# Hybrid decoder step, expert layer: shorter routing, ranked experts with their own capacities, outputs scattered to tokens' places

## What is computed

```python
lg = (t @ w_rg) + b_rg                      # 4 groups
g = argmax(lg); p_top = softmax(lg)[g]
le = (t @ w_re[g]) + b_re[g]                # 4 experts of the group
top_v, top_i = top_k(le, 2)
w2 = softmax(top_v) * p_top
hid = silu(t @ w_gate[e]) * (t @ w_up[e])   # 1024 -> 256, 16 experts
out = sum over the two experts of w2 * (hid @ w_down[e])
x = x + out;  y = rmsnorm(x)
```

## Time and profile before

| | us |
|---|---|
| median of 3 runs | 1096.22 (1095.71 to 1102.13) |
| the profiled execution | 1102.08 |
| its span, first to last instruction | 1100.3 |
| PE busy | 881.9 (80%) |
| DVE busy | 661.7 (60%) |
| ACT busy | 426.6 (39%) |
| POOL busy | 230.9 (21%) |

### The profile page before, as it was taken

One profiled execution on the slowest core, in us unless ns is written; L12 is line 12 of the kernel. 1 busy time (PEld: TensorE's weight loads), 2 busy tenths in 40 slices (PEclk: granted clock), 3 DMA queues, 4 the chain that ended last, 5 costly groups with the idle time before them and its releaser, 6 DMA issues.

```text
span 1100.3 us, 16526 instructions
## 1 busy us (share of the span) xinstructions
PE 881.9 (80%) x6294; PEld 569.4 (52%) x6294; DVE 661.7 (60%) x1001; ACT 426.6 (39%) x744; POOL 230.9 (21%) x174
## 2 busy tenths in 40 slices
PE   5999897698899999648999699801899999999500
PEld 3766442264566443326666355401777887787300
DVE  5614754848655301767883333385488888888266
ACT  5420211545504101546664223460364555464121
POOL 2108965404120000300000000043111011100053
PEclk9999997889979999688999899955899999999855
DMA  8237763000212488400001222192688889872275
GB/s 299 43 95 243 245 214 125 0 25 15 61 60 78 146 260 286 164 8 1 2 1 39 77 77 79 40 311 76 226 304 296 288 300 323 287 273 99 73 269 183
DMA packets 100533, 164.78 MB, mean 150 GB/s; under 512 B 12954, under 2 KB 62634, under 8 KB 100466
## 3 DMA queue, kind: packets, MB, share of 16 engines
q1 hardware_dynamic: 92642, 138.10, 37.9%
q0 software_dynamic: 6208, 22.09, 6.1%
q10 hardware_dynamic: 1616, 3.70, 0.9%
HBM read 136.36 MB, written 27.51 MB: 149 GB/s over the span
## 4 chain that ended last, share of the span: by engine, by line
PE 56%; DVE 20%; issue 6%; ACT 5%; DMA 5%; POOL 4%; SPq 3%; POOLq 0%; ACTq 0%; DVEq 0%
PE ps L1933 15%; PE ps L1934 14%; PE ps L1935 14%; DVE w_reg L1323 2%; POOL kv L796 2%; DVE mxs L1585 2%; PE ps L2210 2%; DVE kv L1742 1%; ACT hT_reg L1213 1%; PE ps L2107 1%; DMA w_reg<-y_scratch,yrow 1%; PE ps L2282 1%; POOL rst L824 1%; SPq L630 1%; PE ps L2074 1%
## 5 line engine op out<-in xcount | busy, mean ns | idle before, releaser
L1933 PE MATMUL ps<-hT_reg,w_reg 128*128 128x344 f16 (+1 forms) x312 | 99.7, 319 | 4.6 <-DVE hT_reg L1335 2.7
L1933 PE MATMUL ps<-hT_reg,mix_reg 128*128 128x208 f16 x384 | 98.7, 257 | 4.8 <-DVE hT_reg L1815 4.8
L1934 PE MATMUL ps<-hT_reg,w_reg 128*128 128x344 f16 (+1 forms) x312 | 99.6, 319 | 0.0
L1935 PE MATMUL ps<-hT_reg,w_reg 128*128 128x344 f16 (+1 forms) x312 | 99.3, 318 | 0.0
L1934 PE MATMUL ps<-hT_reg,mix_reg 128*128 128x208 f16 x384 | 98.7, 257 | 0.0
L1935 PE MATMUL ps<-hT_reg,mix_reg 128*128 128x208 f16 x384 | 98.6, 257 | 0.0
L796 POOL TENSOR_TENSOR kv<-kv,mix_reg 128x1024 f32<-128x1024 f32 x32 | 82.4, 2604 | 47.8 <-DMA kv<-in_cache_k 47.8
L1933 PE MATMUL ps<-w_reg,hT_reg 128*128 128x512 f16 (+1 forms) x216 | 83.7, 387 | 4.9 <-DVE w_reg L1323 3.2
L1934 PE MATMUL ps<-w_reg,hT_reg 128*128 128x512 f16 (+1 forms) x216 | 83.4, 386 | 0.0
L1935 PE MATMUL ps<-w_reg,hT_reg 128*128 128x512 f16 (+1 forms) x216 | 83.1, 385 | 0.0
L824 POOL TENSOR_TENSOR rst<-rst,neghalf 128x1 f32<-128x1 f32 (+3 forms) x27 | 18.9, 702 | 254.9 <-DVE rst L1573 254.9
(11 more groups left out here) (376 smaller groups left out, 2245.5 us busy)
## 6 DMA issues: line engine op xcount, KB each, us to landing
kv<-in_cache_k SPq DMA_DIRECT2D x64, 256.0 KB, 3.4
w_reg<-in_w_gate SPq DMA_DIRECT2D x16, 1024.0 KB, 5.6
w_reg<-in_w_up SPq DMA_DIRECT2D x16, 1024.0 KB, 8.2
w_reg<-in_w_down SPq DMA_DIRECT2D x16, 1024.0 KB, 10.6
w_reg<-in_w_in SPq DMA_DIRECT2D x12, 1024.0 KB, 6.8
mix_reg<-in_cache_v SPq DMA_DIRECT2D x32, 256.0 KB, 3.2
kv<-in_cache_v SPq DMA_DIRECT2D x32, 256.0 KB, 3.1
y_scratch<-kv SPq DMA_DIRECT2D x16, 512.0 KB, 4.0
```

What stands on the lines that cost most here:

```text
L1933: pe.matmul(out, lh, rh, start=start, stop=False)
L1934: pe.matmul(out, lh, rl, start=False, stop=False)
L1935: return pe.matmul(out, ll, rh, start=False, stop=stop)
```

## The change

In words, by place:

- **Output projection**: SyncE loads gate and up of expert 0 before it; ScalarE rounds them at tiles 2 and 5, VectorE splits them at tiles 3 and 8. GpSimd splits only gate and up of expert 1. The constants of routing are made at tile 7.
- **Routing**: no mask of valid tokens, one product for both choices, `r_a16` in f16; prefix sums over tiles by ten matmuls (`strict16`, `ones16`) into one PSUM bank; place and column come out of one number `r_q`; gates, overflow counts and `oexp` come after the token table, behind the first token reads. The token table holds t+1 for a first choice and -(t+1) for a second; `tok` is its absolute value, `dest` the row in `y_scratch` (2 x 1032 rows).
- **Ranking**: experts 0 to 2 stay first at capacity 208; the other 13 are ranked by count in slots of capacity 212, 200, 188, 176, 164, 152, 140 and six of 128 (one part only); SyncE reads their numbers from `sexp`.
- **Slots**: written out, no loop; all widths by `CAPS[e]`; sigmoid as exp, ln, exp on ScalarE in place of plus one and reciprocal on VectorE; one part, 12 matmuls, of down where the capacity is 128; GpSimd stores y by indirect DMAs, `scatter`.
- **The end**: y lies by token, so SyncE loads it by plain DMAs; GpSimd has only the powers left.

```diff
+FIXED = 3
+CAP_TOP, CAP_STEP = 212, 12
+CAPS = [208] * FIXED + [max(P, CAP_TOP - CAP_STEP * j) for j in range(NE - FIXED)]
+def parts(e):
+    return [(0, P), (1, more(e))] if more(e) > 0 else [(0, P)]
@@ SyncE
+            sp.wait_ge(s_wol, KC // 2)
+            load_gate_up(0)
...
+            for t in range(NT + 1):
+                sp.dma_start(yg[t][0:rows(t)],
+                             yd.rearrange("(c t) d -> t c d", c=2)[P * t:P * t + rows(t)]).then_inc(y_in[t][0], 16)
@@ GpSimd
-            for part in range(2):
-                pool.wait_ge(s_mh2, part + 1)
-                split_first(s_mlo, 0, part)
-            pool.wait_ge(s_mhd, 1)
-            split_first(s_mld, 0, 2)
+            def scatter(e):
+                pool.wait_ge(s_ya, e + 1)
+                pool.wait_ge(s_yv, e + 1)
+                for g, r in parts(e):
+                    pool.indirect_dma_start(out=yd[:, :], out_offset=bass.IndirectOffsetOnAxis(
+                        ap=dest[0:r, 2 * e + g:2 * e + g + 1], axis=0), in_=yb[0:r, e % 2, D * g:D * g + D],
+                        in_offset=None, bounds_check=2 * T - 1, oob_is_err=False).then_inc(s_yo[e % 2], 16)
+            pool.wait_ge(s_rtr, NT + 2)
             gather(0)
             gather(1)
             for part in range(2):
                 pool.wait_ge(s_mh2, part + 3)
                 split_first(s_mlo, 1, part)
-            for e in range(2, NE):
-                gather(e)
+            pool.wait_ge(s_route, 1)
+            for e in range(NE):
+                if e + 2 < NE:
+                    gather(e + 2)
+                scatter(e)
@@ ScalarE, slot
+                    act.activation(g, gate_up(e)[0], ACT.Exp, scale=-ISC2).then_inc(s_sg, 1)
+                    act.wait_ge(s_sg, 3 * e + 1)
+                    act.activation(g, g, ACT.Ln, bias=1.0).then_inc(s_sg, 1)
+                    act.wait_ge(s_sg, 3 * e + 2)
+                    act.activation(g, g, ACT.Exp, scale=-1.0).then_inc(s_sg, 1)
                     if e != NE - 1:
+                        read_tokens(e + 1, 0)
+                        read_tokens(e + 1, 2)
@@ VectorE, routing after the counts
-            for t in range(NT + 1):
-                link(dve.tensor_tensor(r_pos[:, t], r_pos[:, t], r_ne, ALU.add))
-                link(dve.tensor_tensor(r_ne, r_ne, ps[:, 1, 16 * t:16 * t + 16], ALU.add))
+            link(dve.scalar_tensor_tensor(r_key, n_all, float(NE), iof[:, 0:NE], ALU.mult, ALU.subtract))
+            link(dve.tensor_tensor(r_beat[:, 0:nd, 0:nd], r_key[:, FIXED:].unsqueeze(1).to_broadcast([P, nd, nd]),
+                                   r_key[:, FIXED:].unsqueeze(2).to_broadcast([P, nd, nd]), ALU.is_gt))
+            link(dve.tensor_reduce(r_sl[:, FIXED:], r_beat[:, 0:nd, 0:nd], AX, ALU.add))
...
+            link(dve.scalar_tensor_tensor(r_sq, n_pos, SCL, per_expert(r_base), ALU.mult, ALU.add))
+            link(dve.scalar_tensor_tensor(r_sq, r_d, float(CAP_TOP), r_sq, ALU.is_ge, ALU.add))
+            chosen(r_sq, r_q)
@@ VectorE, slot
+                    if e != NE - 1:
+                        read_tokens(e + 1, 1)
+                    dve.wait_ge(s_sg, 3 * e + 3)
...
+                    for g, r in parts(v):
+                        dve.wait_ge(s_down, downs(e - 2) + 2 * g + 2)
+                        ins = dve.tensor_scalar(yb[0:r, v % 2, D * g + 512:D * g + D], ps[0:r, 5 + 2 * g, :], ISC2, None,
+                                                ALU.mult)
+                    ins.then_inc(s_yv, 1)
...
+                if e + 2 < NE:
+                    split_gate_up(e + 2, 0)
+                    split_gate_up(e + 2, 1)
+                if e + 1 < NE:
+                    split_down(e + 1)
@@ TensorE, counts
-            pe.matmul(ps[:, 0, 0:144], strict[:], r_a2, start=True, stop=True)
-            pe.matmul(ps[:, 1, 0:144], ones[:], r_a2, start=True, stop=True).then_inc(s_rc, 1)
+            pe.matmul(ps[:, 6, 0:160], strict16[:], r_a16.rearrange("p t e -> p (t e)"), start=True, stop=False)
+            for t in range(NT + 1):
+                ins = pe.matmul(ps[:, 6, 16 * (t + 1):160].rearrange("p (t e) -> p t e", e=16), ones16[:],
+                                r_a16[:, t].unsqueeze(1).to_broadcast([P, 9 - t, 16]), start=False, stop=t == NT)
+            ins.then_inc(s_rc, 1)
```

More of the change, by code:

```diff
@@ L102, with more, y_sent, downs @@
 PB = 4
+def more(e):
+    return CAPS[e] - P
+def parts(e):
+    return [(0, P), (1, more(e))] if more(e) > 0 else [(0, P)]
+def y_sent(e):
+    return 16 * sum(len(parts(k)) for k in range(e % 2, e + 1, 2))
+def downs(e):
+    return sum(2 * len(parts(k)) for k in range(e + 1))
+def one_bank(e):
+    return 4 * CAPS[e] <= 512
 def unit_banks():
@@ L478, in build @@
         r_tmp = work(18, 16)
-        r_a, r_pos = work(9, 16), work(9, 16)
-        r_ne, r_oc, r_inc, r_ost = [work(16) for _ in range(4)]
+        r_beat = r_tmp[:, 0:16]
+        r_d, r_sq, r_w = [work(9, 16) for _ in range(3)]
+        r_a16 = work(80).bitcast(F16).rearrange("p (t e) -> p t e", t=10)
+        r_key, r_sl, r_capm, r_base, r_oc, r_inc, r_ost, r_se = [work(16) for _ in range(8)]
         r_thr = work(8)
@@ L483, in build @@
         r_cmj = work(NOV, 16)
-        r_r, r_e, r_o, r_g, r_f, r_q, r_p, r_c, r_po, r_co, r_x, r_y = [work(18) for _ in range(12)]
-        r_q3 = work(18, 8)
-        r_tv = work(18)
+        r_q, r_qc, r_tv = [work(18) for _ in range(3)]
+        r_v, r_neg, r_none = [work(COLS) for _ in range(3)]
+        iof_p = work(P)
+        iof_c = work(COLS)
         oneh_p = work(18 * P // 2).bitcast(F16).rearrange("p (n q) -> p n q", n=18)
@@ L562, in when_overflow @@
                 body()
-        def run_slots(eng, slot):
-            for e in range(3):
-                slot(0, e, e)
-            with eng.Fori(1, NE // 2 - 2) as i:
-                slot(i, 1)
-                slot(i, 2)
-            for e in range(NE - 3, NE + 1):
-                slot((e - 1) // 2, e - 2 * ((e - 1) // 2), e)
         block = ctx.enter_context(nc.Block())
@@ L1257, in overflow @@
+            split_down(0, 16)
+            act.wait_ge(s_mw[1], 32)
+            for dst, src, _ in expert_parts(1, 0)[0:2]:
+                act.activation(dst, src, ACT.Copy, scale=SC)
+                act.activation(src, src, ACT.Copy, scale=SC).then_inc(s_mh2, 1)
+            read_tokens(0, 0)
+            read_tokens(0, 2)
+            for e in range(NE + 1):
+                slot(e)
             def overflow():
@@ L1773, in _ @@
[L1773 to L1781 removed]
+            link(dve.tensor_scalar(r_ost, r_ost, float(P), 1.0 - CAP_TOP, ALU.mult, ALU.add))
@@ L2266, in _, with transpose_tokens @@
+            ins.then_inc(s_rc, 1)
             for n in range(18):
+                r = rows(n % 9)
                 pe.wait_ge(s_rs1, n // 9 + 1)
-                ins = pe.matmul(ps[:, 2, 0:COLS], oneh_p[:, n], oneh_c[:, n], start=n == 0, stop=n == 17)
+                ins = pe.matmul(ps[:, 7, 0:COLS], oneh_p[0:r, n], oneh_c[0:r, n], start=n == 0, stop=n == 17)
             ins.then_inc(s_rsu, 1)
-            pe.wait_ge(s_route, 1)
-            def transpose_tokens(s, loaded, e4, e2):
-                pe.wait_ge(s_gx[s], loaded)
+            def transpose_tokens(e):
+                s, c, r = e % 2, CAPS[e], more(e)
+                pe.wait_ge(s_gx[s], y_sent(e))
```

629 lines of the change are left out of this document (332 added, 297 removed).

## The result

Four runs of the changed kernel took 1178.65 to 1183.31 us, median 1182.36, beside 1096.47 for the kernel before: a ratio of 1.0755, 95% interval 1.0709 to 1.080. The change costs 86 us. I had forecast slower, and 1113 us; the measured time lies 50 us above the upper end of my range.

What follows compares the result with a forecast made beforehand. Slots were taken as bound by TensorE, routing as a VectorE chain. Routing -27.3, slots +58.8 and the end -14.9 sum to +16.6 us, 1118.7 for the profiled execution, scaled to 1113 us; 8-in-10 range 1050 to 1132.

Steps and rivals of the forecast that it cites:

- What bounds the kernel: Kernel before: routing is one chain on VectorE; expert slots are bound by TensorE, at work 239 of 255 us.
- the routing chain: Routing on VectorE: first gather at 733.8 instead of 758.5, -24.9 us; -27.3 up to the second expert's gate and up end.
- its cost of 0: Output projection: the added copies and splits cost 0, since TensorE sets the pace; 4 us if the cover were gone.
- The loop through GpSimd: Slots: scatters queued ahead of gathers close a loop; a large slot takes 23.2 us instead of 16.05, +58.8 in all.
- Y: In a slot, the end of VectorE's last read of y, forecast 10.4 us after the transposes' start.
- scatters end at 3.1 and 5.3, the first gather at 7.5, the second starts at 7.8 and lands 5.0 later at the least: Large slot, GpSimd's queue after VectorE's last y read, slowed by its splits: rows land 12.8 us after that read.
- Y + 15: Large slot: the gather's landing if weight loads delay it, 15 us after VectorE's last y read instead of 12.8.
- slots 2 to 8: The seven slots with two scatters and two gathers in the loop, 23.2 us each, 162.4 us together.
- The end: From the last expert's gate and up to the kernel's end: shorter down, plain loads of y; -14.9 us from 79.
- (a): Slots: GpSimd's order binds but VectorE's splits do not block it; -29.4 us in total, 1067 us, chance 0.30.
- (b): Slots: gathers land in time and TensorE stays the bound; -69.6 us in total, 1027 us, chance 0.12.
- (c): Slots: only one or two of four indirect DMAs blocked, 21 us each, +40; about 1095 us, no change, chance 0.06.

Runs made afterwards that it cites:

- part 1: The changed kernel with GpSimd issuing the gather of expert e+4 ahead of the scatter of expert e: 1033.4 us, ratio 0.9378.
- Part 2: The changed kernel with VectorE's three splits held back until GpSimd has issued the slot's scatters and gathers: 1111.65 us, ratio 1.0107.
- part 9: Four separate edits to the changed kernel, to VectorE's or GpSimd's order around the first scatter: 1188.87, 1178.87, 1175.22 and 1185.46 us.
- Part 3: The changed kernel with SyncE issuing a slot's weight loads only after its gathered rows have landed: 1139.72 us, ratio 1.0372.
- part 7: The kernel of part 1 with ScalarE's first token read moved behind the first of the sigmoid's three functions: 1023.2 us, ratio 0.931.
- the first run: The kernel of part 1, gathers ahead of scatters, 1033.4 us; with every capacity 208 instead of the ranked ones it took 1088.39 us.

## Why the prediction was right in sign and wrong in size

*What bounds the kernel, and the routing chain: right.* The first gather came 28.0 us earlier, 4.1 of them from earlier in the execution: 23.9 gained against 24.9 forecast (its own sum, 758.5 less 733.8, gives 24.7; the listed operations behind the counts add up to 8.3 us and not 7.8, and took 7.6).

```profile
730.52 1.35 POOL L901 DMA_INDIRECT hT_reg<-h_scratch,tok  x1 [23.07 <-DVE tok L1848]
```

From the last router logits to it are 16.4 us, in the kernel after and in every run below, where it was 41.7 before: 25.3 gained. The output projection took 126.6 us instead of 125.2, but 125.0 to 126.7 in the other runs with the same work beside it, so its cost of 0 holds. No 16-element operation of the chain takes 4 us any more.

*The loop through GpSimd: right.* `scatter(e-1)` ahead of `gather(e+2)` closes the loop, and part 1 opens it with one edit: 149 us. Y came 10.8 us after the start of the transposes (10.4 forecast), and the granted clock of 0.77, against 0.98 before, comes with a TensorE that stands 12 us a large slot.

*The step that failed: "scatters end at 3.1 and 5.3, the first gather at 7.5, the second starts at 7.8 and lands 5.0 later at the least".* The path is right, and two of its terms were sized wrong.
- One split for each scatter. My rows had a DMA behind one lone VectorE operation, and I assumed that GpSimd would be let in at the end of each. In slots of two parts it was let in after three: the last gather starts at Y + 10.4, not 7.8. Part 2 shows that the splits do it: 1.03 us with them held back. Why three and not one stays open (part 9).
- The landing. I had written "the weight loads, issued at Y + 4.4 and 6.6, can make that Y + 15", and put it into the range but not into the sum. They were issued between Y + 5 and Y + 7.5, and the last gather landed 9.5 us after its start. Part 3 shows it: 5.0 us with the loads behind it, 43 us of the time.

With both, and 0.4 us for Y, a large slot is 30.7 us by the prediction's own sum (23.2 + 0.4 + 2.6 + 4.5), and 31 was measured in this one. Over the 14 slots the excess is 63.7 us: 32.2 in slots 2 to 8 (194.6 instead of 162.4), 17.7 in 9 to 11, 13.8 in the last four. I was also off by one slot at both ends. The gather of expert k stands behind the scatter of expert k - 3, so the loop begins with expert 3: the first of my seven slots has no scatter to wait for and took 18.9 us, not 23.2, which hides 4 us of the error. The pattern of slots of one part sets in one slot later, and the last slot, which I gave no gather, waits for one too (16.1 instead of 11).

*The end: right,* 65.9 us against 64.1.

*The rivals.* (a) is refuted: VectorE's splits do block GpSimd, also in the f16 form. Nor did its 1067 come in part 2, where the scatters are not blocked: 1112, since there the splits and the weight loads wait in their place. (b) is the time of part 1 within 1%, with the bound at TensorE that it names. (c) erred the other way, like my forecast: not fewer blocked DMAs, but longer blocks.

*The Trainium skill,* "SBUF — State Buffer", section "Who interferes with whom": its rule that an operation of VectorE with two SBUF inputs contends with a GpSimd instruction that reads SBUF agrees with 6.63 against 1.03 us in part 2. Its inferred addition is that `tensor_tensor`, since it takes the read interface only, didn't stall DMAs whose descriptors GpSimd writes; that inference does not carry over to the indirect DMAs here beside SCALAR_TENSOR_TENSOR. No run here tells whether they wait to read their index column or to write descriptors.

*The range* took my own "Y + 15" as its far end, and so held one error and not two of the same sign in the same slot: the last gather landed at Y + 19.9 (10.4 and 9.5) in the slot shown.

The version of part 7 beats both kernels: 1023.2 us, 6.9% less than before. What the change gains in routing (25.3 us) and by smaller capacities (55 us in the first run) is real; no run separates the sigmoid's three functions or the split beside the projection as gains. The order of gathers and scatters on GpSimd took all of it away.

## What to carry to other kernels

When work moves into the queue of an engine that also issues the loads of the next stage, ask of each entry what it waits for: a store that waits for the end of a stage must not stand in front of a load that could start at its beginning. A price taken from one blocked operation is not that of the same operation in front of a run of three, and what is issued in the same moment (here 3 MB of weights) belongs into the sum, not only into the range. A loop through several engines multiplies every such error by its number of rounds, so count first which rounds are in the loop.

## What the runs showed of the hardware

- An indirect DMA that GpSimd started beside VectorE's splits of 128x2048 ended 0.9 us after the end of one split (2.24 us in all) or of three back to back (6.63 us, 6.65 with a memset of one column between them). Unhindered it took 0.9 to 1.1.
- Whether it is let in after one split or after three differs between slots of one part and of two, alike in every profiled execution with this order of splits; I found no reason.
- A gather of 208 rows, issued within 6 us behind three loads of 1 MB, landed 9.5 us after the start of its second half; issued ahead of them, after 5.0 (part 3) and 4.8 (part 2).
- Eight loads of 1 MB and a small one in flight did not delay the first: 6.8 us until the first sum, 7.0 with two.
- Three kernels with the same instructions up to there (parts 1, 7 and the one with the end's loads two at a time) started the first gather at 731.5, 727.5 and 724.5 us. The difference is there before the output projection (589.9, 585.4 and 583.1), so a gain of a few us in the later stages is read better from a fixed point in the trace than from the time of the whole.
